# Copies ahead of exponentials, rescaling ahead of maxima, and no work on masked key blocks in a fused transformer kernel

## The reference

```
w = softmax(where(mask, q @ k.T, -inf)); out = w @ v        # per head, 128 queries at a time
```

## Time and profile before

| | us |
|---|---|
| median of 3 runs (2812.62 to 2821.64) | 2815.7 |
| the profiled execution, by its own time | 2820.83 |
| its span in the trace | 2819.1 |
| TensorE busy, 90% of the span | 2527.8 |
| VectorE busy, 54% | 1529.4 |
| ScalarE busy, 32% | 903.9 |

### The profile page before, as it was taken

One profiled execution on the slowest core, in us unless ns is written; L12 is line 12 of the kernel. 1 busy time (PEld: TensorE's weight loads), 2 busy tenths in 40 slices (PEclk: granted clock), 3 DMA queues, 4 the chain that ended last, 5 costly groups with the idle time before them and its releaser, 6 DMA issues.

```text
span 2819.1 us, 42055 instructions
## 1 busy us (share of the span) xinstructions
PE 2527.8 (90%) x17582; PEld 2023.7 (72%) x17582; DVE 1529.4 (54%) x2533; ACT 903.9 (32%) x1563; POOL 76.5 (3%) x148
## 2 busy tenths in 40 slices
PE   8999999899997889638886899998999997888998
PEld 6677778588875666238874688876788875556998
DVE  5656475555544655674446555545555453564554
ACT  2331131422222433612313422222322223343543
POOL 0000000000000000000000000000000000000000
PEclk9999999999999999768988999999999998999999
DMA  7235436334343111000002244443344432101543
GB/s 279 88 114 200 179 107 222 106 141 142 135 149 137 60 31 45 0 2 4 4 4 90 82 138 146 139 151 122 127 137 140 148 136 76 45 30 46 179 180 135
DMA packets 55773, 309.74 MB, mean 110 GB/s; under 512 B 5921, under 2 KB 9377, under 8 KB 28065
## 3 DMA queue, kind: packets, MB, share of 16 engines
q1 hardware_dynamic: 32944, 224.74, 22.3%
q0 software_dynamic: 20736, 75.51, 8.0%
q10 hardware_dynamic: 1904, 6.80, 0.6%
HBM read 305.98 MB, written 1.05 MB: 109 GB/s over the span
## 4 chain that ended last, share of the span: by engine, by line
PEld 40%; PE 30%; issue 11%; DVE 11%; ACT 7%; DMA 1%; PEldq 0%; DVEq 0%; ACTq 0%; SPq 0%
PEld bank L1246 13%; PEld bank L1239 13%; PEld bank L1242 12%; PE bank L1119 4%; PE bank L1298 4%; PE bank L1116 2%; PE bank L1178 2%; PE bank L1194 2%; PE bank L1092 2%; PE bank L983 2%; PE bank L990 2%; PE bank L986 2%; ACT hn L1628 2%; PE bank L1073 1%; DVE stats L2206 1%
## 5 line engine op out<-in xcount | busy, mean ns | idle before, releaser
L2052 DVE TENSOR_TENSOR w_lo<-ring,w_hi 128x1024 fp32r<-128x1024 f32 (+1 forms) x198 | 236.2, 1193 | 450.7 <-ACT w_hi L1593 450.6
L1242 PE MATMUL bank<-ffn_x_lo,w_hi 128*128 128x512 f32 x1008 | 399.6, 396 | 0.0
L1246 PE MATMUL bank<-ffn_x_hi,w_lo 128*128 128x512 f32 x1008 | 399.6, 396 | 0.0
L1239 PE MATMUL bank<-ffn_x_hi,w_hi 128*128 128x512 f32 x1008 | 399.6, 396 | 0.0
L1593 ACT ACTIVATE w_hi<-ring 128x1024 fp32r<-128x1024 f32 (+1 forms) x198 | 203.7, 1029 | 289.9 <-PE bank L1242 278.6
L1984 DVE SCALAR_TENSOR_TENSOR ms<-mod_rows,c_silu 128x1024 f32<-128x1024 f32 x200 | 243.9, 1220 | 1.2
L1246 PEld LDWEIGHTS bank<-ffn_x_hi,w_lo 128*128 128x128 f32 x1008 | 189.9, 188 | 46.3
L1239 PEld LDWEIGHTS bank<-ffn_x_hi,w_hi 128*128 128x128 f32 x1008 | 189.9, 188 | 46.3
L1242 PEld LDWEIGHTS bank<-ffn_x_lo,w_hi 128*128 128x128 f32 x1008 | 189.8, 188 | 46.3
L1239 PE MATMUL bank<-ffn_h_hi,w_hi 128*128 128x512 f32 x528 | 211.7, 401 | 0.0
L1246 PE MATMUL bank<-ffn_h_hi,w_lo 128*128 128x512 f32 x528 | 209.3, 396 | 0.0
(11 more groups left out here) (436 smaller groups left out, 4723.3 us busy)
## 6 DMA issues: line engine op xcount, KB each, us to landing
ring<-in_stream SPq DMA_DIRECT2D x211, 1024.0 KB, 4.8
mod_rows<-in_mod_stream POOLq DMA_DIRECT2D x144, 512.0 KB, 3.8
one_const<-in_one ACTq DMA_DIRECT2D x1, 1665.0 KB, 13.2
mix_const<-in_two ACTq DMA_DIRECT2D x1, 1440.0 KB, 6.1
win_const<-in_win ACTq DMA_DIRECT2D x1, 1089.0 KB, 5.0
x<-in_x SPq DMA_DIRECT2D x4, 256.0 KB, 4.6
c_silu<-in_c SPq DMA_DIRECT2D x1, 1024.0 KB, 9.8
x<-in_x SPq DMA_DIRECT2D x1, 1024.0 KB, 24.9
```

The lines of the kernel that those rows point to most:

```text
L1239: mm = pe.matmul(bank[:, 0:tok], w_high, hi, start=k == 0, stop=False)
L1242: mm = pe.matmul(bank[:, 0:tok], w_high, lo, start=False, stop=False)
L1246: mm = pe.matmul(bank[:, 0:tok], w_low, hi, start=False, stop=last)
L2052: V.tensor_tensor(low[:, 0:h.nk, :], raw_half(h), high[:, 0:h.nk, :].bitcast(F32), ALU.subtract).then_inc(sem("w_split"), 1)
```

## The change

It has three parts.

1. Key blocks that a mask shuts out altogether are left out. A diff, fox or dilated unit with t = 0 is 2 x 128 wide, one with t = 1 stays 2 x 256; a window unit is 384 wide. Scores, transposes, products with v, exponential, copy, maximum and rescaling shrink with it.
2. The mask is added in place in the bank, and only where it does something: on the last key block of a part in diff and fox, on the first 128 of 384 columns in window, on everything in dilated. The buffer `s` is not used any more; maximum and exponential read the bank, and ScalarE frees it after the exponential, where VectorE freed it after the mask.
3. In each step ScalarE copies the transposed probabilities of unit i-2 ahead of the exponential of unit i. VectorE rescales unit i-1 ahead of the maximum of unit i, in the mixers always, and in the blends in the first unit after other work (`fresh`).

```diff
@@ scalar, attention step
                 def step(i):
                     if i < n:
+                        b, use = turns.next()
+                    if 2 <= i < n + 2:
+                        u = us[i - 2]
+                        bank, free = full_bank()
+                        nc.scalar.activation(u.bufs["pT"][:, (i - 2) % 2, 0:u.width], bank[:, 0:u.width], ACT.Copy).then_inc(sem("pT_ready"), 1)
+                        act.wait_ge(sem("pT_ready"), b_t + i - 1)
+                        act.nop().then_inc(free, 1)
+                    if i < n:
                         u = us[i]
-                        b, use = turns.next()
                         act.wait_ge(sem("max_ready"), b_max + i + 1)
...
-                        if u.mask is None:
-                            last.then_inc(bank_free[b], 1)
-                            act.wait_ge(bank_free[b], use + 1)
-                            act.nop().then_inc(sem("exp_ready"), 1)
-                        else:
-                            last.then_inc(sem("exp_ready"), 1)
-                    if 2 <= i < n + 2:
-                        u = us[i - 2]
-                        bank, free = full_bank()
-                        nc.scalar.activation(u.bufs["pT"][:, (i - 2) % 2, :], bank[:, :], ACT.Copy).then_inc(sem("pT_ready"), 1)
-                        act.wait_ge(sem("pT_ready"), b_t + i - 1)
-                        act.nop().then_inc(free, 1)
+                        last.then_inc(bank_free[b], 1)
+                        act.wait_ge(bank_free[b], use + 1)
+                        act.nop().then_inc(sem("exp_ready"), 1)
@@ vector, attention
-                        src = bank[:, 0:u.width]
+                        src = bank[:, 0:u.width].rearrange("p (k w) -> p k w", k=u.parts)
                         if u.mask is not None:
-                            src = u.bufs["s"][:, i % 2, 0:u.width]
-                            link(V.tensor_tensor(src, bank[:, 0:u.width], u.mask, ALU.add))
-                            dve.nop().then_inc(free, 1)
+                            part = src[:, :, u.mask_at:u.mask_at + u.mask.shape[2]]
+                            link(V.tensor_tensor(part, part, u.mask, ALU.add))
...
+                def step(i, fresh):
+
+                    if fresh:
+                        rescaled(i)
+                        largest(i)
+                    else:
+                        largest(i)
+                        rescaled(i)
@@ units, diff (fox and dilated alike) and window
-                        cols = slice(t * P, (t + 1) * P)
-                        sc = [(ph1["q"][64 * a:64 * a + 64, h, cols], ph1["q"][64 * a:64 * a + 64, 4 + h, :], SEQ, [])
+                        cols, keys = slice(t * P, (t + 1) * P), (t + 1) * P
+                        sc = [(ph1["q"][64 * a:64 * a + 64, h, cols], ph1["q"][64 * a:64 * a + 64, 4 + h, 0:keys], keys, [])
...
-                            sc = [(ph4["q"][rows, j, cols], ph4["q"][rows, 8 + j // 4, :], TOK, [])]
-                            pv = [(kt, ph4["v"][:, kt, 64 * kv:64 * kv + 64]) for kt in range(4)]
+                            sc = [(ph4["q"][rows, j, cols], ph4["q"][rows, 8 + j // 4, P:TOK], TOK - P, [])]
+                            pv = [(kt, ph4["v"][:, 1 + kt, 64 * kv:64 * kv + 64]) for kt in range(3)]
```

More of the change, by code:

```diff
@@ L654, in build, with mask_of @@
                 "pair_w": (c4("perm_pair"), c4("cos2"), c4("sin2"))}
-        def both(a):
-            return a.rearrange("p (t n) -> p t n", t=2)
+        def mask_of(table, t, parts, k0, k1):
+            return table.rearrange("p (t n k) -> p t n k", t=2, n=2)[:, t, 0:parts, k0:k1]
         def units_of(kind):
             us = []
+            if kind in ("diff", "fox", "dilated"):
+                table = c1("dilated" if kind == "dilated" else "causal")
             if kind == "diff":
@@ L679, in units_of @@
                             sel = c1("sel").rearrange("p (h n) -> p h n", h=4)[0:4, h, :]
-                            more = [(ph1["cum"][0:4, 1, cols], sel), (sel[:, 0:P], ph1["cum"][0:4, 2, :])]
-                            sc.append((ph1["q"][:, 8 + h, cols], ph1["q"][:, 12 + h, :], SEQ, more))
-                            outs.append((0, P, [(2 * n + kt, ph1["v"][:, kt, (4 + h) * P:(5 + h) * P]) for kt in range(2)]))
-                        us.append(Unit(sc, 2, outs, ph1["o"][:, 4 + 2 * g:6 + 2 * g, cols], mask=both(c1("causal"))[:, t, :], bufs=ph1))
+                            more = [(ph1["cum"][0:4, 1, cols], sel[:, 0:keys]), (sel[:, 0:P], ph1["cum"][0:4, 2, 0:keys])]
+                            sc.append((ph1["q"][:, 8 + h, cols], ph1["q"][:, 12 + h, 0:keys], keys, more))
+                            outs.append((0, P, [(n * (t + 1) + kt, ph1["v"][:, kt, (4 + h) * P:(5 + h) * P]) for kt in range(t + 1)]))
+                        us.append(Unit(sc, 2, outs, ph1["o"][:, 4 + 2 * g:6 + 2 * g, cols], bufs=ph1,
+                                       mask=mask_of(table, t, 2, t * P, keys), mask_at=t * P))
             elif kind == "dilated":
@@ L686, in units_of @@
                     for t in range(2):
-                        cols = slice(t * P, (t + 1) * P)
+                        cols, keys = slice(t * P, (t + 1) * P), (t + 1) * P
                         sc, outs = [], []
                         for n, h in enumerate((2 * g, 2 * g + 1)):
-                            sc.append((ph1["q"][:, h, cols], ph1["q"][:, 8 + h, :], SEQ, []))
-                            outs.append((0, P, [(2 * n + kt, ph1["v"][:, kt, h * P:(h + 1) * P]) for kt in range(2)]))
-                        us.append(Unit(sc, 2, outs, ph1["o"][:, 2 * g:2 * g + 2, cols], mask=both(c1("dilated"))[:, t, :], bufs=ph1))
+                            sc.append((ph1["q"][:, h, cols], ph1["q"][:, 8 + h, 0:keys], keys, []))
+                            outs.append((0, P, [(n * (t + 1) + kt, ph1["v"][:, kt, h * P:(h + 1) * P]) for kt in range(t + 1)]))
+                        us.append(Unit(sc, 2, outs, ph1["o"][:, 2 * g:2 * g + 2, cols], bufs=ph1, mask=mask_of(table, t, 2, 0, keys)))
             elif kind == "gqa":
@@ L1081, in step @@
                         pe.wait_ge(sem("p_ready"), b_p + i - 1)
-                        for kt in range(4):
+                        for kt in range(u.width // P):
                             mm = pe.transpose(bank[:, kt * P:(kt + 1) * P],
@@ L2148, in blend @@
                     elif what == "unit":
-                        scores(i)
+                        scores(i, before != "unit")
                     elif what != "none":
                         norms(what, i)
+                    before = what
             def gated_add(bank, free, layer, v, c, tok):
```

26 lines of the change are left out of this document (13 added, 13 removed).

## The result

The changed kernel takes 2773.5 us, the median of four runs (2761.75 to 2777.45), against 2818.6 for the kernel before beside it: a ratio of 0.983, with a 95% interval of 0.9807 to 0.9853, 45.1 us less. The forecast was 2771 and 44.4 less. The total came out right. The stages did not: the window stage gave half of its term, and the mixers, gqa and the recurrence, which had no term, gave more than forecast.

What follows compares the result with a forecast made beforehand. TensorE, busy 90% of the span, was taken to bound all but the window stage, where VectorE ends last. Terms 13.0 + 7.3 + 24.1 = 44.4 us off 2815.7 gave 2771; range 2758 to 2787, own range 2763 to 2779.

Steps and rivals of the forecast that it cites:

- Mixers, 13.0: Mixers: leaving out key blocks at t = 0 saves 9.0 us in eight diff or dilated units, 4.0 in two fox units.
- rival (c): Clock falls after the first window group's stall and in fox units go away: 8 us faster, 2763; chance 0.08.
- the loss of 4.5: Mixer 1: if waits for VectorE's norms grow by what TensorE saves there, 4.5 of the 13.0 us are lost.
- Order in gqa, 7.3: gqa: copying and rescaling first removes TensorE's waits for copies and shortens those for rescaling, 7.3 us; bounds 4 and 8.
- VectorE's durations: Window units on VectorE: mask 0.29 us, maximum 0.13 less, rescaling 0.07 less; a unit falls from 2.84 to 2.24 us.
- Rival (b): VectorE's writes into PSUM are dear, 0.4 us more at each of 32 window masks: some 8 us, 2779; chance 0.08.
- Window, 24.1: Window stage: 14.5 us from five groups, 2.7 from the first group, 6.9 from the last eight units and drain.
- rival (d): Longer waits beside less TensorE work hold the clock at 0.50 through the window stage: 2855; chance in full 0.01.
- A milder form: Window stage: one clock fall of 1.4 us in every group, 2779, inside the forecast's own range; no separate chance given.
- The prediction's own sign of being wrong: Wrong if masks stayed near 0.69 us, TensorE awaited bank_free in mixers, or the clock fell in several window groups.
- The bank held longer, 0: Banks freed later cost nothing; without about 0.6 us of cover at odd diff units, under 1 us at three places.
- Rival (a): Only removed work counts, order does not: gqa's 7.3 and some 5 of window's 24.1 fall away, 2783; chance 0.09.

Runs made afterwards that it cites:

- the control: Two thrown-away matmuls of 384 columns ahead of each window group's rotary product, against the changed kernel with both orders undone: 2815.6 us, ratio 0.9993.

## Why the prediction was right, and where it was not

By its sum, in the order of its steps; "measured" are the three profiles of the changed kernel against the two of before.

- **Mixers, 13.0.** Measured to the end of mixer 1: 431.1 and 430.3 before, 414.6, 413.0 and 412.4 after, so 16 to 19. Two things are in it. Against the one profile of the kernel with the orders alone, where the fox units run at full clock as they do after (mixer 1 ends at 426.2), the blocks give 11.6 to 13.8: the term holds. The other 4 to 5 us are the fox units' falls of the clock, which the prediction had only as a part of rival (c). In none of the three profiles did they fall, nor in the two kernels with the new order alone. The waits of the earlier trace rows are 3.6 us after, 4.0 before, so the loss of 4.5 that was put beside this term did not come.
- **Order in gqa, 7.3.** Measured 8.7 to 9.2 (160.5 and 160.1 to 151.2 to 151.4). The waits went from 17.1 us to 9.9, 7.2, which is the term. The rest is in part the slow stretch behind the long wait: in the dense half behind it the matmuls were back at full pace within 0.6 us of its start, where before it took 2.3 (1.7 in the second profile).
- **VectorE's durations.** 295 ns for the mask in the bank (taken: 0.29), 557 for the maximum (0.56), 420 for the rescaling (0.42). The write into the bank, for which no row stood, costs as much as one into SBUF: 693 ns for 512 columns in place in a bank, 688 into the buffer before. Rival (b) is out. Its price was also added up wrongly: three units in each of five groups and the last row's eight are 23 masks, not 32. The maxima over a bank show no extra cost either: 557 ns for 384 columns, where 0.56 was taken from the rows of before. The Trainium skill states a higher fixed cost for PSUM ("VectorE: DVE Perf Modes", section on the TRN2 errata); the measured rows don't bear it out, with 685 ns from a bank and 686 from SBUF over 512 columns.
- **Window, 24.1.** At full clock the term holds closely: a group 3.13 less (2.9 taken), the first one 2.61 (2.7), the last row 7.06 (6.9), the stage 25.3 from 148.2 to 122.9. In that are 1.4 for a fall before, and against it 1.4 lost in the dense half behind the first group, which ran longer at the lower clock (7.4 us where it had taken 5.9 and 6.1); so the part of rival (c) that hoped for the stall did not come. In the first profile the stage gave 12.7. The step that failed is rival (d): it set the long form, a clock at 0.50 through the whole stage, at 0.01, and held against it that 1.69 us of waiting had left the clock at 1.00 in the earlier trace rows. That row was read as if such a wait were safe, and one group stood for all: the fifth group of the same trace lost its clock behind the same wait of 1.69 us. With the thinner units, waits of 1.27 to 1.74 let it fall too, and at 1.74 in most places. A milder form was priced at 1.4 a group, which is what a fall cost before; with units of 384 columns it costs 1.5 to 3.5 in a group, and 7.5 in the last row, where no dense half brings the clock back. That was not seen. The prediction's own sign of being wrong, a granted clock that falls in more than one window group, did come in the first profile.
- **The bank held longer, 0.** No wait for a bank shows in the three profiles.
- **Rival (a)**, only removed work counts: the orders alone gave 13.4, the blocks alone 15.5. Out; if anything, it is the other way round.
- **The total.** The first pair of profiles: 16.5 from the mixers, 9.1 from gqa, 12.7 from the window stage, 8.8 from the recurrence and what follows it up to the window stage, and -0.2 elsewhere, 46.9. The sum was 13.0, 7.3 and 24.1. So the terms at full clock were right, and that the forecast also hit the total was luck: an unforeseen loss of 12 met 4 to 5 us from the fox units, some 2 in gqa, and some 9 of chance in one profile. In the second pair of profiles, without falls in the window stage, it is 17.3, 8.9 and 25.4, and 53.7 in all.

## What to carry to other kernels

Read a saving on TensorE together with the waits that stay inside the thinned stretch: less work around the same wait can cost the clock, and then all of the saving, above all in a long row of light steps with no dense product behind them. Price each part of a change at full clock, and say beside it what one fall costs and where it would be made good. Where a long wait can't be taken away, throw-away matmuls in it are a test of the cause, if they stand in the wait itself; they gave 24 us in the kernel with the orders undone, and in the changed kernel no gain clear of the noise. Moving the waited-for engine's other work behind the stretch shortens the groups by 1.46 us each; in the total it showed only together with the filling of the last row's waits.

## What the runs showed of the hardware

- A wait of TensorE between scores, transposes and products with v was or was not followed by a fall to the lower clock. Counted over groups 2 to 6 and the last row, six places in a profile: with a wait of 1.69 us and units of 512 columns 4 of 18 (two profiles of before, and ScalarE's order alone), with waits of 1.86 to 2.22 and units of 512 4 of 6 (the orders alone), with 1.74 and units of 384 10 of 12 (blocks alone, and the control), with 1.27 and units of 384 3, 0 and 0 of 6 (three profiles of the changed kernel), with the same waits covered 0 of 12. At nearly the same wait, 1.69 and 1.74, the thinner units fell much more often; no experiment changed the width alone. What decides between the outcomes of one and the same wait was not found.
- With units of 512 columns the clock came back by itself, among scores, transposes and products with v, in 7 of 8 falls, 2.9 to 9.9 us after it had gone. With units of 384 columns it never did so in 14 falls, though TensorE was hardly idle: it stayed down up to the next dense or rotary product, or into the drain of the last row. In the first profile's last row TensorE was busy 23.2 of 23.7 us at a granted clock of 0.57, and the clock was back only for the last 2.5 us, when the scores were over (12 records of products in 1.58 us, where 6 had taken 1.54):

```profile
2498.80:2522.50 23.70, 23.20 (x81) 13.48 (x80) 11.82 (x41) 12.78 (x42) 0.00 (x0) 0.57 0.00 0
```

```profile
2520.51 1.58 PE L1096 MATMUL bank<-win_pT,win_v 128*64 128x128 f32 x12
```

  In the groups, the clock was back within 1 to 4 us of the start of the dense products behind them. The Trainium skill, "TensorE: Matmul & The Clock Gate", part on PE-mode transposes, says that transposes don't count as busy in the same way; the first of these rows agrees as far as it goes, but the scores and the products with v, 3 of a unit's 3.88 us, did not bring the clock back either, and in the drain it came back among transposes and products.
- The fox units of mixer 0 lost the clock in both profiles of before (0.87 between 150 and 190 us) and once in each of three profiles with the exponential ahead of the copy (0.96), but in only one of eight with the copy first (0.91 there, 1.00 in the others). TensorE shows no wait of a unit there in either kind. Whether the copy's place does it, and how, stays open.
